# Hybrid decoder trunk on one core: expert rows added to the output in DRAM by accumulating scatters, and a third probability buffer in attention

## The chip, the core and the metric

The kernel runs on one core of a Trainium2 chip. The core has a matrix engine (PE, TensorE), a vector engine (DVE), an activation engine (ACT), GpSimd (POOL), a queue engine for transfers (SP) and 16 DMA engines. The metric is the device time of one execution in microseconds; less is better. POOL's indirect DMAs take one index per partition and move one row of DRAM for each.

## The reference

Two layers over 1024 tokens of width 1024, float32. Cut to what matters:

```python
for l in range(DEPTH):                                   # DEPTH = 2
    z = rms_norm(x, norm1_gain[l]) @ w_in[l]             # q | k | v | u, 512 columns each
    q, k = per-head RMSNorm, partial rotary              # 8 heads of 64
    att = dilated_attention(q, k, v)                     # causal, a count mask, softmax
    pool = pool_mixer(u, w_pool[l], pool_scale[l])
    x = x + concat(att, pool) @ w_out[l]
    h = rms_norm(x, norm2_gain[l])
    x = x + hier_moe(h, ...)     # each token goes to 2 of 16 SwiGLU experts (256 wide), with weights
```

## The kernel before

Tokens lie in T = 8 tiles of 128 (`x_res`, called `xr` in the code). One program runs over both layers in a hardware loop. Each engine has its own instruction stream, in order, written out by hand; semaphores tie them. Stages of a layer:

- **Input projection.** PE turns normalised x and multiplies with `w_in`, first q and v for the 8 tiles, then k and u. ACT squares a tile (`square_x`), DVE makes the factor and scales (`norm_x`), PE transposes (`xt`), DVE applies the gain and splits it into a high and a low part (`gain1`). A projection of a tile and half is 24 matmuls (L1321). For the second layer the first of this is done inside the last stage of the layer before.
- **Attention.** 8 heads x 8 row tiles = 64 steps m. PE `scores(m)` (L1381, L1383), DVE `mask(m)` (L1025: adds the mask, finds the row maximum, writes buffer `pr[m % 2]`), ACT `exp(m)` (L730, in place), PE `probs_t(m)` transposes (L1301), ACT and DVE copy the turned blocks from PSUM (L748, L1035), PE `probs_v(m)` multiplies with 128 columns of v, those of two heads (L1407), DVE `over_sum(m)` divides the 64 columns of its head (L1041, L1044). `mask(m)` waits until `probs_t(m - 2)` is done. At steps 3 and 11 of every 16, DVE splits q and k of the next head (`q_and_k_low`, L1000, L1003); ACT writes the high part of k twice (L673, L677).
- **Output projection**, residual into `xr`; ACT writes the normalised rows to `token_rows` in DRAM. Then the **router**, whose sorting is done by DVE and by small float16 matmuls (L1504).
- **Experts.** Tokens are sorted by expert into blocks of 128 rows. There is room for BLOCKS = 31; the first layer uses 22, the second 23, a number known at run time (`used`), and the engines branch past the rest one by one. For block t POOL gathers rows (L579), PE transposes, multiplies with gate and up (L1527) and down (L1540). ACT and DVE copy y to SBUF, and ACT writes it to `y_table` in DRAM (L816). POOL also gathers for the unused blocks.
- **Combination.** After the last block POOL gathers two rows of `y_table` per token (L595, 16 gathers per layer) and DVE adds them into `xr` with the token's weights (L1267, L1269). In layer 2 POOL then writes `xr` to the output (L601).

The instructions at the end of a layer's expert stage are these:

```python
for t in range(T):
    if t >= GATHS:
        pool.wait_ge(x_ready, upto(l + 1, T, t - GATHS + 1))
        pool.sem_inc(s_passed, 1)
    for k in range(2):
        pool.indirect_dma_start(
            out=gath[t % GATHS][:, k, :], out_offset=None,
            in_=y_table, in_offset=bass.IndirectOffsetOnAxis(ap=pos_i[:, k, t:t + 1], axis=0),
        ).then_inc(s_gath[t % GATHS], 16)
```

## Time and profile before

| | |
|---|---|
| median of 3 runs | 1771.88 us (1771.16 to 1774.53) |
| the profiled execution: its own time, its span | 1771.18 us, 1769.1 us |
| PE busy | 1488.7 us, 84% |
| DVE busy | 829.6 us, 47% |
| ACT busy | 470.7 us, 27% |
| POOL busy | 273.9 us, 15% |
| moved by DMA | 228.42 MB, mean 129 GB/s |
| mean granted TensorE clock | 0.932 of full |

The span runs from the first to the last instruction. The shares are means over stages with different limits. Input projection, output projection and expert blocks keep PE near full; the attention leaves some of its time, and two stretches without much PE work stand at the end of each layer's expert stage.

### The profile page before, as it was taken

How to read it: one execution, taken by the hardware profiler on the slowest of the kernel's cores; microseconds unless marked ns; L12 is line 12 of the kernel's file. 1: busy time of each engine (PE TensorE's matmuls, PEld its weight loads, DVE VectorE, ACT ScalarE, POOL GpSimd, SP SyncE). 2: the span in 40 equal slices, each digit the busy share in tenths (PEclk: the TensorE clock that was granted, in tenths of full speed). 3: DMA queues.
4: the chain of work that ended last, by engine and by line, in shares of the span. 5: the costliest groups of instructions: out<-in, count | busy, mean ns of one | idle time of the engine just before them, and what ended most of it. 6: DMA issues, size and time to landing. Idle time of an engine off the chain costs nothing.

```text
span 1769.1 us, 23000 instructions
## 1 busy us (share of the span) xinstructions
PE 1488.7 (84%) x6931; PEld 1068.9 (60%) x6932; DVE 829.6 (47%) x2097; ACT 470.7 (27%) x904; POOL 273.9 (15%) x259
## 2 busy tenths in 40 slices
PE   2999987998992999998269999789999659999960
PEld 2887867886882444444158787678778524444430
DVE  3778667664436112221377866766634441222114
ACT  3222155763111011111212313566512101111100
POOL 1200049002001001110310000940200020111114
PEclk8999989999995999999579999899999869999985
DMA  8410020000057588942740002000001935888637
GB/s 304 154 43 1 0 96 1 1 1 1 36 179 260 173 297 290 367 155 83 246 166 0 1 0 81 16 1 1 1 13 48 329 99 196 293 294 297 226 128 288
DMA packets 118497, 228.42 MB, mean 129 GB/s; under 512 B 6184, under 2 KB 72816, under 8 KB 118416
## 3 DMA queue, kind: packets, MB, share of 16 engines
q1 hardware_dynamic: 90352, 129.55, 21.5%
q0 software_dynamic: 18128, 65.71, 10.4%
q10 hardware_dynamic: 9936, 32.14, 4.5%
q8 instruction: 44, 0.72, 0.2%
q14 instruction: 37, 0.30, 0.1%
HBM read 183.33 MB, written 44.04 MB: 129 GB/s over the span
## 4 chain that ended last, share of the span: by engine, by line
PE 71%; DVE 11%; issue 8%; DMA 4%; ACT 4%; ACTq 0%; POOL 0%; DVEq 0%; PEld 0%; POOLq 0%; SPq 0%; PEldq 0%
PE ps L1527 18%; PE ps L1321 17%; PE ps L1301 9%; PE ps L1454 9%; PE ps L1540 8%; PE ps L1407 4%; PE ps L1468 2%; DMA arena<-token_rows,next_tok 1%; DMA big<-y_table,pos_i 1%; DVE arena L1025 1%; DVE w_in_lo L920 1%; ACT arena L730 1%; ACT arena L748 1%; DVE arena L1122 1%; PE ps L1381 1%
## 5 line engine op out<-in xcount | busy, mean ns | idle before, releaser
L1301 PE MATMUL ps<-cst,arena 128*128 128x128 f32 x1682 | 244.5, 282 | 128.5 <-DVE arena L891 59.8
L1527 PE MATMUL ps<-big,arena 128*128 x720 | 326.3, 607 | 11.0 <-issue 10.5
L1301 PEld LDWEIGHTS ps<-cst,arena 128*128 128x128 f32 x1682 | 201.3, 145 | 206.8 <-DVE arena L891 61.9
L881 DVE TENSOR_TENSOR arena<-ps,par 128x512 f32<-128x512 f32 x126 | 81.2, 686 | 365.5 <-PE ps L1301 365.3
L1527 PEld LDWEIGHTS ps<-big,arena 128*128 128x128 f32 x720 | 135.9, 194 | 172.5 <-issue 172.5
L1321 PE MATMUL ps<-w_in_hi,hT_hi 128*128 128x512 f32 x512 | 207.1, 404 | 12.3 <-DVE w_in_lo L920 8.6
L1321 PE MATMUL ps<-w_in_hi,hT_lo 128*128 128x512 f32 x512 | 203.0, 396 | 0.0
L1321 PE MATMUL ps<-w_in_lo,hT_hi 128*128 128x512 f32 x512 | 202.9, 396 | 0.0
L1540 PE MATMUL ps<-big,arena 128*128 x360 | 165.3, 603 | 7.0 <-issue 7.0
L1407 PE MATMUL ps<-big,arena 128*128 128x128 f32 x1152 | 150.6, 276 | 0.0
L1407 PEld LDWEIGHTS ps<-big,arena 128*128 128x128 f32 x1152 | 140.0, 193 | 1.3
L578 POOL COPY next_tok<-row_tok 128x1 int32 (+1 forms) x62 | 14.8, 238 | 781.0 <-PE ps L1301 452.2
L730 ACT ACTIVATE arena<-arena,st 128x128 f32<-128x128 f32 (+7 forms) x128 | 99.1, 774 | 82.1 <-DVE st L1025 81.2
L1321 PEld LDWEIGHTS ps<-w_in_hi,hT_hi 128*128 128x128 f32 x512 | 98.8, 193 | 34.8 <-DVE w_in_lo L920 10.4
L1025 DVE CUSTOM_DVE_ANT_0 arena<-ps,cst 128x128 f32<-128x128 f32 (+7 forms) x128 | 96.5, 754 | 44.7 <-PE ps L1301 40.7
L1321 PEld LDWEIGHTS ps<-w_in_hi,hT_lo 128*128 128x128 f32 x512 | 98.2, 192 | 21.4
L1540 PEld LDWEIGHTS ps<-big,arena 128*128 128x128 f32 x360 | 66.1, 194 | 73.9 <-issue 73.9
L1321 PEld LDWEIGHTS ps<-w_in_lo,hT_hi 128*128 128x128 f32 x512 | 98.6, 193 | 19.6
L1454 PE MATMUL ps<-w_o_hi,cat_hi 128*128 128x512 f32 x256 | 102.9, 402 | 7.4 <-DVE cat_lo L1087 7.4
L1454 PE MATMUL ps<-w_o_hi,cat_lo 128*128 128x512 f32 x256 | 100.3, 392 | 0.0
L1454 PE MATMUL ps<-w_o_lo,cat_hi 128*128 128x512 f32 x256 | 100.2, 391 | 0.0
L1381 PE MATMUL ps<-k_high,q_parts 128*128 128x512 f32 (+1 forms) x192 | 82.0, 427 | 12.0 <-DVE k_low L1003 11.8
(159 smaller groups left out, 1749.5 us busy)
## 6 DMA issues: line engine op xcount, KB each, us to landing
big<-in_w_gate SPq DMA_DIRECT2D x32, 1024.0 KB, 8.8
big<-in_w_up SPq DMA_DIRECT2D x32, 1024.0 KB, 11.3
big<-in_w_down SPq DMA_DIRECT2D x32, 1024.0 KB, 13.5
y_table<-arena ACTq DMA_DIRECT2D x45, 512.0 KB, 6.8
big<-in_w_in SPq DMA_DIRECT2D x18, 1024.0 KB, 10.4
big<-in_w_out SPq DMA_DIRECT2D x4, 2048.0 KB, 10.1
token_rows<-arena ACTq DMA_DIRECT2D x16, 512.0 KB, 2.8
y_table<-x_res POOLq DMA_DIRECT2D x15, 512.0 KB, 9.5
```

Of the source, the lines that this page charges most:

```text
L730: sc.activation(pr[b][:, 0:nk], pr[b][:, 0:nk], ACT.Exp, scale=-1.0, bias=st[:, 64 + m % 16:65 + m % 16], accum_out=st[:, 80 + m % 16:81 + ...
L748: sc.activation(prT[b][:, 0:nb, :], ps[:, 4, 0:nb * P] .rearrange("p (a c) -> p a c", c=P), ACT.Copy).then_inc(pt0_ev, 1)
L881: ins = ve.tensor_tensor(out=dst[:, 4 * h:4 * h + 4, :], in0=ps[:, banks + h, :].rearrange("p (a c) -> p a c", c=P), in1=spread(gain[:, 4 ...
L1025: ve.tensor_tensor_reduce(out=pr[b][:, 0:nk], in0=ps[:, 2 * b:2 * b + 2, :].rearrange("p a c -> p (a c)")[:, 0:nk], in1=cst[:, C_MASK + SE ...
L1301: ins = te.transpose(ps[:, bank + i // 4, (i % 4) * P:(i % 4 + 1) * P], src, ident)
L1321: ins = te.matmul(ps[:, 2 + 2 * par_ + i, :], a[par_][:, k, :], b[:, k, :], start=k == 0 and n == 0, stop=k == K - 1 and n == 2)
L1381: te.matmul(ps[:, 2 * b + c // 512, 0:w], q_parts[a][:, i * P:(i + 1) * P], k_high[a][:, c:c + w], start=True, stop=False)
L1407: ins = te.matmul(ps[:, 6 + b, 0:P], prT[b][:, j, :], v[:, j, p * P:(p + 1) * P], start=j == 0, stop=j == i)
L1454: ins = te.matmul(ps[:, 2 * par_ + h, :], a[par_][:, k, :], b[:, k, :], start=k == 0 and n == 0, stop=k == K - 1 and n == 2)
L1468: ins = te.matmul(ps[:, 6 + par_, 0:P], h2T[par_][:, k, :], wr_all[:, ds(l * (K * NR) + k * NR, P)], start=k == 0, stop=k == K - 1)
L1527: ins = te.matmul(ps[:, 2, :], xgT[:, k, :], big[:, ds(at + k * 2 * FE, 2 * FE)], start=k == 0, stop=k == K - 1)
L1540: ins = te.matmul(ps[:, 4 + h, :], aT[:, k, :], big[:, ds(at + (E_GU + k * D + 512 * h), 512)], start=k == 0, stop=k == 1)
```

## The change

Four things change together.

1. `y_table` and the combination go. While the output projection runs, ACT also writes each tile of x to the output in DRAM. For each block j POOL issues `add_rows(j)`: an indirect DMA that adds the 128 rows of y to the rows of their tokens in the output (rows without a token go to spare rows behind it). It stands 5 blocks after the gather in POOL's order, for all 31 blocks. Since a token has two experts, `y_whole` lets the add of a used block start only after the one before it has landed. The weights go into the experts: DVE cuts the weights into three parts of 11 bits, 16 float16 matmuls of 96 columns sort them by row, and `act` is multiplied by them.
2. The gathered rows `xg` and `y` now lie in tiles 2 to 7 of `xr`. For layer 2 SP loads tiles 0 and 1 of x from the output after the add of the last block with tokens has landed (`x_whole`), and tiles 2 to 7 after all 31 adds.
3. Attention has three `pr` buffers, so that `mask(m)` waits for `probs_t(m - 3)`. `probs_v` multiplies with the 64 columns of its own head, and the 8 tiles of a head lie in one PSUM bank; `over_sum` runs once per head, on 512 columns.
4. The second copy of k's high part moves from ACT to DVE. `in_low(l + 1, 0)` moves behind the first `rows_evac`.

```diff
-GATHS = 4
+AHEAD = 5
+OUT_ROWS = SEQ + ROWS
-        att = A[:, 2048:3072].rearrange("p (t c) -> p t c", c=P)
+        att = kT_r.rearrange("p (a t c) -> p a t c", a=PAIRS, c=P)
-        pr = ring(5120, SEQ)
+        pr = ring(5120, SEQ) + [A[:, 2048:3072]]
-        xg = ring(0, D, RING)
+        xg = [xr[:, 2 + i, :] for i in range(RING)]
-        y = ring(4864, D, RING)
+        y = [xr[:, 2 + RING + i, :] for i in range(RING)]
...
+                with sp.If(l > 0):
+                    sp.wait_ge(x_whole, upto(l, 1, 0))
+                    sp.sem_inc(s_passed, 1)
+                    for t in range(2):
+                        sp.dma_start(xr[:, t, :], out[t * P:(t + 1) * P, :]).then_inc(s_again[t], 16)
+                    for t in range(2):
+                        sp.wait_ge(s_again[t], l * 16)
+                        sp.sem_inc(x_ready, 1)
...
+                    sp.wait_ge(s_add, upto_added(l, 0))
+                    sp.sem_inc(s_passed, 1)
+                    for t in range(2, T):
+                        sp.dma_start(xr[:, t, :], out[t * P:(t + 1) * P, :]).then_inc(s_again[t], 16)
...
-                    ch.link(nc.gpsimd.tensor_copy(next_tok[:, slot:slot + 1], row_tok[:, ds(j, 1)]))
                     pool.indirect_dma_start(
                         out=xg[slot], out_offset=None, in_=token_rows,
-                        in_offset=bass.IndirectOffsetOnAxis(ap=next_tok[:, slot:slot + 1], axis=0)).then_inc(s_xg[slot], 16)
+                        in_offset=bass.IndirectOffsetOnAxis(ap=row_tok[:, j:j + 1], axis=0)).then_inc(s_xg[slot], 16)
+                def add_rows(j):
+
+                    pool.wait_ge(y_whole, upto(l, BLOCKS, j + 1))
+                    pool.sem_inc(s_passed, 1)
+                    pool.indirect_dma_start(
+                        out=out, out_offset=bass.IndirectOffsetOnAxis(ap=row_dst[:, j:j + 1], axis=0),
+                        in_=y[j % RING], in_offset=None, compute_op=ALU.add).then_inc(s_add, 16)
...
+                for j in range(BLOCKS):
+                    load_rows(j, j % RING, j // RING)
+                    if j >= AHEAD:
+                        add_rows(j - AHEAD)
+                for j in range(BLOCKS - AHEAD, BLOCKS):
+                    add_rows(j)
+            pool.wait_ge(s_add, upto_added(DEPTH, 0))
...
+                    a_.dma_start(out[ds(t * P, P), :], xr[:, t, :]).then_inc(s_base, 16)
...
                     a_.wait_ge(y1_ready, upto(l, BLOCKS, t + 1))
-                    a_.dma_start(y_table[ds(t * P, P), :], y[slot]).then_inc(s_y[slot], 16)
+                    if not first(t):
+                        a_.wait_ge(s_add, upto_added(l, t))
+                    a_.sem_inc(y_whole, 1)
...
                         moe_down(t, slot, m)
+                        a_.wait_ge(s_add, upto_added(l, t + 1))
+                        a_.sem_inc(x_whole, 1)
                     with a_.Else():
                         a_.sem_inc(y1_ready, 1)
-                        a_.sem_inc(s_y[slot], 16)
+                        a_.sem_inc(y_whole, 1)
...
-                                     in1=k_high[a][own, :].bitcast(f32), op=ALU.subtract).then_inc(staged, 1)
+                                     in1=k_high[a][own, :].bitcast(f32), op=ALU.subtract)
+                    ve.tensor_copy(k_high[a][other, :], kT[own, p, :]).then_inc(staged, 1)
...
-                    if m >= 2:
-                        j = m - 2
+                    if m >= 3:
+                        j = m - 3
...
+                    ve.tensor_tensor(out=att[:, p, :, HD * a:HD * (a + 1)],
+                                     in0=ps[:, 6 + a, :].rearrange("p (t c) -> p t c", c=HD),
+                                     in1=spread(r, HD), op=ALU.mult).then_inc(o_ev, 1)
...
-                        ins = te.matmul(ps[:, 6 + b, 0:P], prT[b][:, j, :], v[:, j, p * P:(p + 1) * P],
-                                        start=j == 0, stop=j == i)
+                        ins = te.matmul(ps[:, 6 + hd % 2, i * HD:(i + 1) * HD], prT[b][:, j, :],
+                                        v[:, j, hd * HD:(hd + 1) * HD], start=j == 0, stop=j == i)
```

Engine POOL, end of a layer's expert stage, before: the last gather of an unused block, then the gathers of the combination.

```order
L574 REGISTER_ALU
L575 ISA
L578 COPY next_tok<-row_tok 128x1
L579 DMA arena<-token_rows,next_tok 128x1024
L588 ISA x2
L595 DMA big<-y_table,pos_i 128x1024 x8
L592 ISA
L595 DMA big<-y_table,pos_i 128x1024 x2
```

The same place of the change; L607 is the gather, L615 the accumulating scatter (its index buffer is in the arena), L613 a wait for `y_whole`.

```order
L603 REGISTER_ALU
L607 DMA x_res<-token_rows,row_tok 128x1024
L615 DMA out_x<-x_res,arena 4992x1024
L603 REGISTER_ALU
L604 REGISTER_ALU
L607 DMA x_res<-token_rows,row_tok 128x1024
L615 DMA out_x<-x_res,arena 4992x1024 x3
L613 REGISTER_ALU
L615 DMA out_x<-x_res,arena 4992x1024
```

The copy of the index and the 16 gathers of `y_table` are gone, and every gather but the first five has a scatter behind it.

Engine DVE, attention, from the mask of a row tile of 256 columns to that of 512 columns, before: each step has a reciprocal and a product of 64 columns.

```order
L1025 ISA arena,st<-ps,cst 128x256
L1025 ISA st 128x1
L1041 RECIPROCAL st<-st 128x1
L1044 TENSOR_SCALAR arena<-ps,st 128x64
L1023 REGISTER_ALU
L1025 ISA arena,st<-ps,cst 128x384
L1025 ISA st 128x1
L1041 RECIPROCAL st<-st 128x1
L1044 TENSOR_SCALAR arena<-ps,st 128x64
```

The same stretch of the change, up to the division of the head before.

```order
L1044 ISA arena,st<-ps,cst 128x256
L1044 ISA st 128x1
L1042 REGISTER_ALU
L1044 ISA arena,st<-ps,cst 128x384
L1044 ISA st 128x1
L1042 REGISTER_ALU
L1044 ISA arena,st<-ps,cst 128x512
L1044 ISA st 128x1
L1061 RECIPROCAL st<-st 128x8
L1063 TENSOR_TENSOR big<-ps,st 128x8x64
```

Sixteen small instructions of a head have become two.

Engine PE, attention, the products with v between two scores, before and then in the change: only the shape of the moving operand differs, from 128 to 64 columns.

```order
L1301 MATMUL ps<-cst,arena 128x128 x4
L1395 REGISTER_ALU
L1301 MATMUL ps<-cst,arena 128x128 x4
L1407 MATMUL ps<-big,arena 128x128 x7
L1377 REGISTER_ALU
```

```order
L1332 MATMUL ps<-cst,arena 128x128 x4
L1426 REGISTER_ALU
L1332 MATMUL ps<-cst,arena 128x128 x4
L1438 MATMUL ps<-big,arena 128x64 x7
L1408 REGISTER_ALU
```

The number of matmuls and their place among the others stay.

## Rows read from the trace of the kernel before

**Rows 1.** Busy time by stretch: length; PE, PEld, DVE, ACT, POOL; clock; DMA.

```profile
238.00:408.00 170.00, 144.07 (x1066) 129.44 (x1065) 113.42 (x306) 112.07 (x227) 67.37 (x31) 0.97 0.05 20
571.50:830.20 258.70, 254.24 (x740) 122.48 (x740) 49.49 (x87) 28.45 (x64) 25.16 (x44) 0.99 0.66 234
830.20:916.50 86.30, 32.31 (x109) 23.79 (x110) 41.80 (x78) 15.63 (x24) 21.05 (x26) 0.67 0.55 193
1706.00:1769.10 63.10, 5.12 (x8) 2.03 (x8) 21.45 (x18) 1.24 (x3) 24.56 (x32) 0.58 0.68 251
```

**Rows 2.** Chain that ended last, by time, between the layers: start, length, what.

```profile
842.08 9.87 DMA arena<-token_rows,next_tok
...
855.30 8.20 DMA big<-y_table,pos_i
...
916.45 12.75 PE ps L1321 x48
```

**Rows 3.** Timeline between the layers: start, length, engine, line, operation.

```profile
839.38 0.60 ACT L813 ACTIVATE arena<-ps 128x512 f32<-128x512 f32 x1 [7.55 <-PE ps L1540]
...
840.65 0.96 POOL L579 DMA_INDIRECT arena<-token_rows,next_tok  x1 [0.50 <-POOL next_tok L578]
...
847.03 1.28 ACT L852 ACT_TABLE_LOAD   x1 [7.04 <-DVEq L1248]
...
866.17 1.06 ACT L625 ACTIVATE arena<-x_res 128x1024 f32<-128x1024 f32 x1 [17.64 <-DVE x_res L1269]
...
875.33 0.79 PE L1321 MATMUL ps<-w_in_hi,hT_hi 128*128 128x512 f32 x1 [3.67 <-DVE hT_lo L909]
```

**Rows 4.** The chain in layer 1, from the second half of tile 0 on.

```profile
43.19 12.49 PE ps L1321 x48
57.00 10.91 PE ps L1321 x48
```

**Rows 5.** Timeline of the end of layer 2.

```profile
1716.03 0.96 POOL L579 DMA_INDIRECT arena<-token_rows,next_tok  x1 [0.50 <-POOL next_tok L578]
```

**Rows 6.** Stretches near the end, columns as in rows 1.

```profile
1732.00:1740.00 8.00, 0.00 (x0) 0.00 (x0) 7.11 (x6) 0.00 (x0) 4.58 (x5) 0.50 1.01 397
...
1757.00:1761.00 4.00, 0.00 (x0) 0.00 (x0) 0.00 (x0) 0.00 (x0) 0.00 (x0) 0.50 0.60 247
```

**Rows 7.** DMA issues of the page: count, KB each, median us to landing.

```profile
y_table<-arena ACTq DMA_DIRECT2D x45, 512.0 KB, 6.8
...
x_res<-in_x SPq DMA_DIRECT2D x1, 512.0 KB, 3.3
arena<-token_rows,next_tok POOLq DMA_INDIRECT x62, 5.9
```

**Rows 8.** Groups of the attention of layer 1 (240 to 408 us): busy, mean ns.

```profile
L1407 PE MATMUL ps<-big,arena 128*128 128x128 f32 x546 | 71.5, 276 | 0.0
L1407 PEld LDWEIGHTS ps<-big,arena 128*128 128x128 f32 x546 | 66.3, 193 | 0.6
...
L1044 DVE TENSOR_SCALAR arena<-ps,st 128x64 f32<-128x64 f32 x62 | 17.6, 284 | 18.8 <-DVE st L1041 14.8 <-PE ps L1407 2.5
...
L1003 DVE TENSOR_TENSOR k_low<-big,k_high 64x1024 fp32r<-64x1024 f32 x8 | 12.1, 1513 | 0.1
...
L1041 DVE RECIPROCAL st<-st 128x1 f32<-128x1 f32 x62 | 9.8, 158 | 0.0
```

**Rows 9.** What PE waited for there: total us, times, longest.

```profile
PE ps L1301 <- ACT arena L748: 11.2, 21, 1.1
PE ps L1381 <- DVE k_low L1003: 5.9, 1, 5.9
PE ps L1301 <- DVE arena L1035: 5.9, 2, 3.1
```

**Rows 10.** Timeline: products with v, and weight loads of the float16 matmuls.

```profile
315.33 1.95 PE L1407 MATMUL ps<-big,arena 128*128 128x128 f32 x16
...
559.53 0.29 PEld L1504 LDWEIGHTS ps<-arena 128*128 128x128 f16 x8 [11.05 <-DVE arena L1200]
```

More of the change, by code:

```diff
@@ L98, in shape_constants @@
     c[:, C_JJ:C_JJ + P] = np.arange(P)
-    c[:, C_TOK:C_TOK + 2 * T] = np.tile(P * np.arange(T), 2)[None, :] + row
+    c[:, C_TOK:C_TOK + 2 * T] = np.tile(P * np.arange(T), 2)[None, :] + row + 1
     c[:, C_DESC:C_DESC + 4] = 4 - np.arange(4)
@@ L104, in shape_constants @@
     c[:, C_INV:C_INV + 16] = 1.0 / (1.0 + np.arange(16))
+    c[:, C_SPARE:C_SPARE + 32] = SEQ + 1 + P * np.minimum(np.arange(32), BLOCKS - 1)[None, :] + row
     return c
@@ L189, in trunk @@
                 for i in range(SLOTS)]
-        gath = [big[:, AT_K + 2 * D * i:AT_K + 2 * D * (i + 1)].rearrange("p (k n) -> p k n", k=2) for i in range(GATHS)]
         def ring(at, size, n=2, inner=None):
@@ L291, in trunk @@
         routed = sem("routed")
+        gate_parts = sem("gate_parts")
+        gates_listed = sem("gates_listed")
+        y_whole = sem("y_whole")
+        x_whole = sem("x_whole")
         w_loaded = sem("w_loaded")
@@ L320, in trunk @@
         s_xg = [sem(f"s_xg{i}") for i in range(RING)]
-        s_y = [sem(f"s_y{i}") for i in range(RING)]
-        s_gath = [sem(f"s_gath{i}") for i in range(GATHS)]
-        s_out = sem("s_out")
+        s_base, s_add = sem("s_base"), sem("s_add")
+        s_again = [sem(f"s_again{t}") for t in range(T)]
         s_ms = sem("s_ms")
@@ L509, in _ @@
                         .then_inc(s_wr, 16)
-            for j in range(2 * SEQ // P, BLOCKS):
-                pool.dma_start(y_table[j * P:(j + 1) * P, :], xr[:, 0, :]).then_inc(s_fill, 16)
             with pool.Fori(0, DEPTH) as l:
@@ L608, in _ @@
             for s in (params, q_high_in, k_high_in, win_top, gain_in, sd1, sqz_done, sdz, cat_top, v_copied, u_copied, t_evac, p_ready, pt0_ev, at_ev, sd2,
-                      ge_exp, dm_exp, silu_done, aT_ready, y1_ready):
+                      ge_exp, dm_exp, silu_done, aT_ready, y1_ready, y_whole, x_whole):
                 a_.sem_inc(s, BIAS)
-            for s in s_y + s_tok:
+            for s in s_tok:
                 a_.sem_inc(s, 1)
@@ L672, in k_top @@
                     own, other = heads(a)
-                    sc.activation(k_high[a][own, c], kT[own, p, c], ACT.Copy)
-                def k_top_again(p, a, c=slice(0, SEQ)):
-                    own, other = heads(a)
-                    sc.activation(k_high[a][other, c], kT[own, p, c], ACT.Copy).then_inc(k_high_in, 1)
+                    sc.activation(k_high[a][own, c], kT[own, p, c], ACT.Copy).then_inc(k_high_in, 1)
                 def in_act(t, par_, h):
@@ L749, in _ @@
                                   .rearrange("p (a c) -> p a c", c=P), ACT.Copy).then_inc(pt0_ev, 1)
-                    if p and n == 1:
+                    if p and n == 3:
                         att_evac(p - 1)
@@ L1055, in _ @@
                         mask(m + 2)
-                    if m >= 1:
-                        over_sum(m - 1)
+                    if m >= T and m % T == 1:
+                        over_sum(m // T - 1)
                     if n == 3:
@@ L1215, in _ @@
                 dve.sem_inc(s_passed, 1)
+                dve.wait_ge(s_base, (l + 1) * (16 * T))
+                dve.sem_inc(s_passed, 1)
+                bits = gate_w[:, :, :].rearrange("p k t -> p (k t)").bitcast(i32)
+                ve.tensor_scalar(gate_bits[:, 0, :], bits, 0x7FF, None, ALU.bitwise_and)
+                ve.tensor_scalar(gate_bits[:, 1, :], bits, 11, 0x7FF, ALU.logical_shift_right, ALU.bitwise_and)
+                ch.link(ve.tensor_scalar(gate_bits[:, 2, :], bits, 22, None, ALU.logical_shift_right))
+                ch.link(ve.tensor_copy(R("parts"), gate_bits[:, :, :].rearrange("p k c -> p (k c)")))
+                parts = R("parts").rearrange("p (k c) -> p k c", k=3)
+                tt(R("tmp3", 32), spread(R("blk"), 32), count, ALU.is_equal)
+                for k in range(3):
+                    ins = ve.tensor_tensor(out=in_gate[:, :, k, :], in0=R("tmp3", 32), in1=spread(parts[:, k, :], 32),
+                                           op=ALU.mult)
+                ins.then_inc(gate_parts, 1)
+                ch.link(ve.tensor_scalar(R("spare"), ps[:, 2, 0:32], 0.0, None, ALU.is_equal))
+                tt(R("spare"), R("spare"), cst[:, C_SPARE:C_SPARE + 32], ALU.mult)
+                ch.link(ve.scalar_tensor_tensor(out=row_dst[:, :], in0=ps[:, 2, 0:32], scalar=-1.0, in1=R("spare"),
+                                                op0=ALU.add, op1=ALU.add))
                 used = dve.value_load(start_i[0:1, NE:NE + 1], min_val=2 * SEQ // P, max_val=BLOCKS)
@@ L1544, in _ @@
                 xtm(0, 0, 0)
+                pe.wait_ge(gate_parts, upto(l, 1, 1))
+                for c in range(2 * T):
+                    ins = te.matmul(ps[:, 7, 0:96], in_row[:, c, :], in_gate[:, c, :, :].rearrange("p k b -> p (k b)"),
+                                    start=c == 0, stop=c == 2 * T - 1)
+                ins.then_inc(gates_listed, 1)
                 used = pe.value_load(start_i[0:1, NE:NE + 1], min_val=2 * SEQ // P, max_val=BLOCKS)
```

149 lines of the change are left out of this document (64 added, 85 removed).

## The prediction, made before the change ran

> **What bounds the kernel now.** I read the stretches first. In the expert blocks PE is busy 254 of 259 us [rows 1], so nothing that other engines save there counts; 22 blocks in 258.7 us are 11.8 us a block, and layer 2 has 23. In the attention PE is busy 144 of 170 us, at a clock of 0.97. Two stretches hold hardly any PE work: 830 to 916 us, between the layers, with 32 of 86 us, and 1706 us to the end, with 5 of 63. Together they last 149 us, and the change works there. Next the chain of waits and the timeline say what these stretches wait for. After the last copy of y (839.4 us) come gathers for unused blocks (842.1 us, 9.9 us to land), a gather of y (855.3 us, 8.2 us), and x is complete when ACT squares it at 866.2 us; the first projection of layer 2 starts at 875.3 us, and the run of 48 matmuls that begins with the second half of tile 1 only at 916.5 us [rows 2, 3]. In layer 1 the run before it starts at 43.2 and this one at 57.0 us, 13.8 us apart [rows 4].
>
> **The gap between the layers.** The last y is copied at 840.0 us. POOL issues the pending gather, now without the copy of its index (840.0 to 841.2; an issue is 0.96 us plus about 0.3 between two), then the scatter of block 21. The trace has no accumulating transfer. Its landing I bound from the write of y (6.8 us) and the gather that took 9.9 us at this very place beside a weight load [rows 2, 7]; I take 8.8, so 850 us. Then ACT sets `x_whole`. SP's loads of tiles 0 and 1 need 3.3 us and a little [rows 7], about 855. But ACT now waits for the scatter before it branches past the unused blocks. That took the 7.0 us between its copy of y and the table load, less about 0.5 to issue the write of y, so 6.5, and lay under the gathers [rows 3]; now it is in the open: 856.5, table load 1.3 and a first operation 0.2, square at 858.0 instead of 866.2. The first projection follows 9.2 us later as before, at 867.2. It takes 7.2 us at the low clock, the transposes 2.0, so the second half of tile 0 starts at 876.4. DVE no longer has 16 additions of 1.28 us between its steps, so I put the spacing of layer 1, 13.8 us, behind it: 890.2 instead of 916.5, a gain of 26 us.
>
> **Tiles 2 to 7 wait for all 31 scatters.** Tile 2 is wanted at about 883, 7 us before that. Nine scatters of unused blocks and three gathers are left at 850. POOL needs 12 x 1.24 = 15 us to issue them. What a scatter occupies of the DMA engines, E, decides more. The engines moved 397 GB/s when full [rows 6]: 512 KB are 1.3 us for a plain copy, the lower end. An add has to read the old row too: twice, 2.6 us. The upper end is the 6.8 us in which a write of y lands [rows 7], as if they went one by one. I take 2.6, nearest to the rows with full engines, since the nine need not wait for each other. Then 851 + 9 x 2.6 + 3 x 1.3 = 878.3, tile 2 at 881.6: just in time, 0 us. At E = 1.3 nothing changes; at 6.8 the last lands at 916, and tile 2 at 919 puts the run at 926, 10 us worse than before.
>
> The Trainium skill (Collectives: The Full Stack, The bandwidth ceiling) says that an add in a DMA engine is slower than a copy not by the addition but by its two source reads, and puts the ratio at two. By it E is 2.6; no row here shows an add, so the sum stands on the bounds above.
>
> **The end.** The last block's scatter is issued behind one gather, at 1716.7 us (the gather stands at 1716.0 now and loses its copy) [rows 5], and lands at about 1723. Eight scatters of unused blocks at 2.6 follow: 1744. Before, data stopped at 1757 + 0.6 x 4 = 1759.4 and the span at 1769.1, 9.7 us later [rows 1, 6]; the same behind 1744 gives 1754, a gain of 15. At E = 1.3 the issues bound it (10 x 1.24, plus 3 to land): 1748, a gain of 21. At 6.8: 1723 + 54 + 10 = 1787, a loss of 18.
>
> **Attention, DVE and ACT.** Gone are 64 reciprocals of 158 ns and 64 products of 284 ns with 18.8 us of idle before them [rows 8], 47 us of DVE's stream per layer; eight divisions of 512 columns (about 0.9 us each with the reciprocal) and eight copies of 64 x 1024 (at most 1.5, as L1003) come back, 19 us. DVE is not the bound, so this counts only where PE waits: 23 us per layer [rows 9]. The 5.9 us before the first score stay and grow by the copy, up to 1.5 us, which ACT had made earlier. The 5.9 us for the copy L1035 come from DVE standing in `q_and_k_low`; the third buffer does not help there. The 11.2 us in 21 waits for ACT's copy do: that copy stands behind `exp(m + 1)`, which waited for a mask that waited for `probs_t(m - 1)`. I take 9.5 of them. Net 8 us per layer, 16 in all; bounds 0 and 23 per layer. The output of attention moves off the arena, which costs nothing.
>
> **Attention, PE.** The product with v streams 64 columns instead of 128. Now 16 of its instructions take 1.95 us, (1.95 - 0.276)/15 = 112 ns apart [rows 8, 10], and 576 per layer are 64 us. If the moving operand sets this, it may halve, 53 ns each, 31 us per layer. If the weight load does, nothing is won. A float32 load lasts 193 ns, and eight float16 loads together 290 ns at the lower clock [rows 8, 10]: a load has a short fixed part, so most of 193 ns is loading, and it fills the 112. I take 0; bounds 0 and 61 us in all.
>
> The Trainium skill (TensorE: Matmul & The Clock Gate, LDWEIGHTS (loading the stationary operand)) gives columns / 1.2 ns, 107 ns for 128 columns whatever the matmul's width. [...]
>
> **The start of the experts.** 16 matmuls of 96 columns come between the first transposes and the first gate matmul: at 1.2 GHz 80 ns each, 1.3 us, plus a wait for DVE's parts, less the index copy that the first gather loses: +1 us per layer, 2 in all. DVE's cutting of the weights (about 4 us) lies under the first gather. The write of x by ACT lies under the output projection. In the blocks the add of one block must land before the next starts: issue and landing of 5.9 to 9.9 [rows 2, 7] fit in 11.8, so 0. POOL's wait for `y_whole` holds up a gather that is wanted three blocks later. If the cover is gone, each us over 11.8 costs 45.
>
> **Sum.** -26 - 15 - 16 + 2 = -55 us against the profiled execution's own 1771.2 (its median of runs is 0.7 higher): **1716 us**.
>
> **Rivals.**
> - *The moving operand sets the pace in attention.* For: the stream is continuous and both explanations give 112 ns. Against: the 193 ns load. Then up to 61 us more: 1655 to 1680. Chance 0.12.
> - *Scatters occupy the engines longer, E = 3.5 to 5.8.* For: the nearest landings are 6 to 7 us. Nine and eight of them stand in the open, so each us of E costs 17: 1731 to 1770. Chance 0.16.
> - *Slower than before.* The same mechanism from E = 5.9 on, where 17 x (E - 2.6) exceeds 55; at 6.8 it gives 1787, and from a landing above 11.8 us the blocks themselves stretch by 45 us per us. Against: full engines moved 397 GB/s. Chance 0.08.
> - *The clock falls in attention*, since half the columns pass; 0.97 now [rows 1]. It was granted 0.5 in stretches without PE work [rows 6]. If a tenth of the 2 x 144 us of PE work ran at 1.2 GHz instead of 2.4, it would cost 29 us: 1745. Chance 0.05.
> - *The tail is not shortened*, because 31 scatters are issued whatever is used: that is the E = 4.5 case, counted above.
> - Forecast, E below 3.5 and no gain on PE: 1698 to 1735. Chance 0.59.
>
> The range reaches from the first rival's middle to the slow scatters' upper part: 1670 to 1758. About 0.2% (3.5 us) is what a measurement can tell from no change. Faster 0.90, within it 0.02, slower 0.08.
>
> **What would show it.** Right: no PE work between about 840 and 867, the square of layer 2 near 858 behind ACT's branches, the run of 48 matmuls near 890; scatters at the end spaced under 3 us and a last stretch of about 48 us; products with v still 112 ns apart; the mask's waits shorter. Wrong: tile 2 of x arriving after 883, ACT waiting for an add inside the blocks, or products with v closer than 100 ns.

## The result, and the profile after

The changed kernel takes 1753.75 us, the median of five executions (1741.32 to 1757.35), against 1771.88: a ratio of 0.9885, 95% interval 0.9867 to 0.9903. So it is faster, by 18 us where 55 were forecast. The profiled execution is the fastest of the five, 1741.3 us (span 1739.4); the working below is held against this one, 29.7 us less span than before. Seven more executions of the same kernel follow in the experiments. All twelve fall into two groups, 1734.6 to 1742.1 (5) and 1750.8 to 1757.4 (7), where all executions of the kernel before (1766.2 to 1774.8) lie within 9 us. That needs a cause of its own.

Busy time by stretch of the kernel after, the same stretches and columns as [rows 1]: attention of layer 1, its expert blocks, the gap, the end.

```profile
238.00:408.00 170.00, 149.15 (x1054) 137.52 (x1052) 102.24 (x199) 103.37 (x217) 63.91 (x31) 0.90 0.05 18
575.00:830.00 255.00, 249.25 (x732) 120.48 (x733) 54.25 (x87) 28.49 (x63) 52.01 (x41) 0.99 0.78 235
830.00:897.90 67.90, 31.95 (x118) 22.50 (x117) 23.01 (x64) 15.66 (x24) 27.82 (x17) 0.72 0.85 225
1676.00:1739.40 63.40, 16.48 (x47) 7.38 (x45) 3.75 (x6) 2.94 (x6) 22.24 (x16) 0.69 0.67 141
```

The gap has shrunk from 86 us to 68. In the attention DVE is relieved (102 us for 113), but PE is busy for 149 us instead of 144, and its mean clock is 0.90 instead of 0.97: PE was made slower, not shorter of work.

I cut both spans at the same events, read from the timelines (start of the first window sum behind the attention, of the last down projection of each layer, of the run of 48 matmuls in [rows 2], end of the last matmul of the projection of layer 2):

| event | before | after | shift |
|---|---|---|---|
| end of layer 1's input projection | 239.9 | 238.9 | -1.0 |
| first window sum, layer 1 | 413.0 | 414.7 | +1.7 |
| last down projection, layer 1 | 826.5 | 829.4 | +2.9 |
| run of 48, layer 2 | 916.5 | 897.9 | -18.6 |
| end of layer 2's input projection | 1101.2 | 1080.8 | -20.4 |
| first window sum, layer 2 | 1275.0 | 1260.4 | -14.6 |
| last down projection, layer 2 | 1702.0 | 1685.8 | -16.2 |
| end | 1769.1 | 1739.4 | -29.7 |

The gap gave 21.5 us (forecast 26), the end 13.5 (15). The two attentions, 173.1 and 173.8 us before, took 175.9 and 179.6: 8.6 us more where 16 less were forecast. That is the miss of this execution.

The chain of the kernel after between the layers (answers to [rows 2]), by start and length:

```profile
829.42 3.45 PE ps L1571 x8
843.87 11.32 DMA out_x<-x_res,arena
...
872.58 8.19 PE ps L1352 x24
...
889.63 4.30 issue
897.88 10.92 PE ps L1352 x48
```

Its timeline there ([rows 3]); the last row is an issue of an add that took 5.88 us:

```profile
856.93 1.58 POOL L615 DMA_INDIRECT out_x<-x_res,arena  x1 [10.20 <-ACTq L851]
...
862.02 1.28 ACT L870 ACT_TABLE_LOAD   x1 [20.02 <-ACTq L850]
...
863.43 1.04 ACT L650 ACTIVATE arena<-x_res 128x1024 f32<-128x1024 f32 x1
...
872.37 5.88 POOL L615 DMA_INDIRECT out_x<-x_res,arena  x1 [0.31 <-issue]
```

The mechanism is the forecast's, a few us late at each step: the last real add lands at 855.2 instead of 850, ACT's square stands at 863.4 instead of 858.0, the first projection at 872.6 instead of 867.2. Tiles 2 to 7 of x come only at some 889, because POOL's first add of an unused block (856.9) waits for ACT's branch, and that for the landing. The sum let these adds start at 850, before ACT had branched.

The end, two rows of POOL's timeline and one of the stretches ([rows 5, 6]):

```profile
1707.94 1.59 POOL L615 DMA_INDIRECT out_x<-x_res,arena  x1 [6.40 <-ACTq L851]
...
1723.66 1.56 POOL L615 DMA_INDIRECT out_x<-x_res,arena  x1 [0.30 <-issue]
...
1730.00:1735.00 5.00, 0.00 (x0) 0.00 (x0) 0.00 (x0) 0.00 (x0) 0.00 (x0) 0.50 1.01 201
```

The engines are full with adds until 1735, 10 us behind the last issue, and move 201 GB/s of payload (182 to 234 in the four stretches of 5 us before), where full engines moved 397 in [rows 6]. By this estimate a 512 KB add occupies all engines for 512 KB / 201 GB/s = 2.6 us: the value taken for E. POOL issues one every 1.87 us, so the engines, not POOL, set the end. The Trainium skill (Collectives: The Full Stack, The bandwidth ceiling) has an add at half a copy's rate; this trace agrees in the main, 201 against 397 GB/s.

In the attention of layer 1 (238 to 408 us), the groups that answer to [rows 8], and the product of 16 of [rows 10]:

```profile
L1438 PE MATMUL ps<-big,arena 128*128 128x64 f32 x546 | 73.6, 284 | 0.0
L1438 PEld LDWEIGHTS ps<-big,arena 128*128 128x128 f32 x546 | 72.1, 207 | 0.7 <-issue 0.2
...
L1023 DVE CAST k_high<-big 64x1024 fp32r<-64x1024 f32 x8 | 11.6, 1453 | 0.1
L1063 DVE TENSOR_TENSOR big<-ps,st 128x512 f32<-128x512 f32 x7 | 4.8, 691 | 0.2
...
338.91 1.90 PE L1438 MATMUL ps<-big,arena 128*128 128x64 f32 x16
```

With half the columns a product still follows the last one after (1.90 - 0.284)/15 = 108 ns (112 before): the weight load sets the pace, so the edit gives PE nothing. What PE waited for (238 to 412 us; answers to [rows 9]):

```profile
PE ps L1332 <- DVE arena L1054: 7.0, 2, 5.3
PE ps L1412 <- DVE k_high L1023: 6.9, 1, 6.9
PE ps L1332 <- ACT arena L765: 4.7, 10, 1.1
```

The waits for ACT's copy fell from 11.2 to 4.7 us. All three together fell from 23.0 to 18.6, and still the attention got 2.8 us longer, so some 7 us went into PE's own work. Stretches of 20 us of the kernel after, two of layer 1 and one of layer 2, show where:

```profile
255.00:275.00 20.00, 17.17 (x98) 16.01 (x96) 10.92 (x18) 7.64 (x18) 18.99 (x11) 0.71 0.00 1
275.00:295.00 20.00, 14.71 (x83) 13.50 (x83) 15.02 (x19) 8.65 (x18) 19.06 (x8) 0.76 0.00 1
...
1155.00:1175.00 20.00, 20.00 (x99) 18.79 (x98) 6.95 (x15) 8.92 (x20) 0.00 (x0) 0.59 0.00 1
```

The next to last column is the DMA share; the one before it the clock. The kernel before had 1.00 and 1.00 in the first two (with 140 and 122 matmuls instead of 98 and 83) and 0.91 at its lowest in layer 2. In the last, PE never stood still and was granted 0.59 of full speed, mostly the lower of its two levels (1.2 instead of 2.4 GHz).

### The profile page after: what moved, and what is told of

It reads as the page before. It is cut to its first block, busy times and chain, and to the rows that moved or that the text cites. A ratio compares the mean times of both kernels' runs of the same rounds, so it can differ in the third digit from the quotient of the medians.

```text
span 1739.4 us, 22561 instructions
## 1 busy us (share of the span) xinstructions
PE 1495.3 (86%) x6963; PEld 1085.7 (62%) x6964; DVE 781.9 (45%) x1883; ACT 454.6 (26%) x886; POOL 314.4 (18%) x204
## 4 chain that ended last, share of the span: by engine, by line
PE 77%; DVE 9%; issue 6%; DMA 3%; ACT 2%; ACTq 1%; POOL 1%; DVEq 0%; SPq 0%; PEld 0%; PEldq 0%; POOLq 0%
PE ps L1558 18%; PE ps L1352 18%; PE ps L1332 10%; PE ps L1485 10%; PE ps L1571 9%; PE ps L1438 6%; PE ps L1412 2%; PE ps L1499 2%; PE ps L1414 2%; DMA out_x<-x_res,arena 1%; DVE k_high L1023 1%; DVE arena L1141 1%; DMA big<-in_w_in 1%; PE ps L1472 1%; DVE w_in_lo L938 1%
## 5 line engine op out<-in xcount | busy, mean ns | idle before, releaser
L1558 PE MATMUL ps<-big,arena 128*128 x720 | 320.5, 598 | 9.8 <-issue 8.4
L1332 PE MATMUL ps<-cst,arena 128*128 128x128 f32 x1242 | 186.6, 285 | 87.3 <-DVE arena L909 46.0
L1558 PEld LDWEIGHTS ps<-big,arena 128*128 128x128 f32 x720 | 133.8, 191 | 167.3 <-issue 167.3
L1332 PEld LDWEIGHTS ps<-cst,arena 128*128 128x128 f32 x1242 | 152.8, 147 | 134.3 <-DVE arena L909 47.6
L607 POOL DMA_INDIRECT x_res<-token_rows,row_tok x62 | 61.0, 984 | 599.2 <-issue 307.7
L1571 PE MATMUL ps<-big,arena 128*128 x360 | 163.8, 598 | 5.4 <-issue 5.4
L1438 PE MATMUL ps<-big,arena 128*128 128x64 f32 x1152 | 154.9, 284 | 0.0
L1438 PEld LDWEIGHTS ps<-big,arena 128*128 128x128 f32 x1152 | 151.9, 207 | 1.5 <-issue 0.4
L615 POOL DMA_INDIRECT out_x<-x_res,arena x62 | 102.7, 1656 | 170.4 <-ACTq L832 140.3
L1571 PEld LDWEIGHTS ps<-big,arena 128*128 128x128 f32 x360 | 65.5, 192 | 71.5 <-issue 71.5
```

The costliest lines, as they stand in the source:

```text
L607: pool.indirect_dma_start(out=xg[slot], out_offset=None, in_=token_rows, in_offset=bass.IndirectOffsetOnAxis(ap=row_tok[:, j:j + 1], axis= ...
L615: pool.indirect_dma_start(out=out, out_offset=bass.IndirectOffsetOnAxis(ap=row_dst[:, j:j + 1], axis=0), in_=y[j % RING], in_offset=None, ...
L1332: ins = te.transpose(ps[:, bank + i // 4, (i % 4) * P:(i % 4 + 1) * P], src, ident)
L1438: ins = te.matmul(ps[:, 6 + hd % 2, i * HD:(i + 1) * HD], prT[b][:, j, :], v[:, j, hd * HD:(hd + 1) * HD], start=j == 0, stop=j == i)
L1558: ins = te.matmul(ps[:, 2, :], xgT[:, k, :], big[:, ds(at + k * 2 * FE, 2 * FE)], start=k == 0, stop=k == K - 1)
L1571: ins = te.matmul(ps[:, 4 + h, :], aT[:, k, :], big[:, ds(at + (E_GU + k * D + 512 * h), 512)], start=k == 0, stop=k == 1)
```

## The experiments

Two theories. **A, the clock:** the products with v stream half the columns, the granted clock falls in the first heads, and this eats the gain. **B, DVE held up beside POOL:** while POOL sums windows and cuts the output weights in the first heads, DVE's pieces of q and k take longer; the change gave DVE one more such piece per head (the copy of k's high part), and PE waits. A third reading, that the scatters or the new end cost the time, is a rival to both. Medians are of five to eight executions unless said; ratios are against the kernel before, run beside them on the same chip (medians 1770.2 to 1772.2).

**1. The changed kernel again** (no edit).

> The changed kernel once more, unedited, for a second profile and the spread of its times. Theory A (the clock falls in attention, because the products with v stream half the columns and PE pauses more): median 1747 to 1755 us, the executions 10 us or more apart, and in the new profile again stretches of the attention at a granted clock under 0.9, not necessarily the same ones. Theory B (fixed stalls in attention, from the second copy of k's high part on DVE): the attention lasts 182 and 186 us again, with the same waits at the same heads, whatever the clock. If the spread comes from the end or the gap instead, the attention is alike in both profiles and the last stretch differs by 10 us.

Median 1739.6 us (1734.6 to 1753.7), ratio 0.9839 (0.9802 to 0.9875). The median lies under A's 1747 to 1755, the executions are 19 us apart as A had it, and B's 182 and 186 us are missed. Clock 0.82, 0.86 and 0.97 from 255 to 315 us, 0.75 in one stretch of layer 2. The attentions took 171.2 and 173.7 us, together 2.0 us less than before, and yet this execution lasted as long as the profiled one above: from the first window sum to the last down projection it took 6.9 us more in the two layers, all of it before the first down projections, where the clock in layer 2 was 0.87 instead of 0.89. The low clock comes again and its depth varies. It lies in the heads beside POOL's work or just behind it: in layer 2 POOL has stopped at 1149.7 us, and the stretch from 1155 to 1175 us has 0.88.

**2. k's second copy back on ACT.** The changed kernel, with

```
-                    ve.tensor_copy(k_high[a][other, :], kT[own, p, :]).then_inc(staged, 1)
...
+                    if n == 10:
+                        k_top_again(p + 1, 0)
```

> The changed kernel with the second copy of k's high part back on ACT. Theory A (clock, from the 64-column products): the waits for that copy go (about 3 to 5 us per layer), the clock still falls somewhere in the attention, the time stays at 1743 to 1755 with the same spread. Theory B (the copy on DVE, stretched from 0.7 to 4 us beside POOL's conversions, stalls PE and the pause then lowers the clock): the attention comes down to about 172 us per layer, the forecast's 8 us of gain, total about 1725 to 1735, spread under 4 us.

1745.5 us (1740.5 to 1760.9), ratio 0.9863: within A's 1743 to 1755, B's 1725 to 1735 missed, the spread stayed. The attentions took 176.5 and 176.1 us, where B had 172. Its timeline in layer 2 shows why the copy is not all of it, DVE and POOL side by side:

```profile
1142.54 9.82 DVE L1031 TENSOR_TENSOR k_low<-big,k_high 64x1024 fp32r<-64x1024 f32 x1
...
1141.53 9.75 POOL L583 TENSOR_TENSOR w_o_lo<-big,w_o_hi 128x4096 fp32r<-128x4096 f32 x1
```

A subtraction of 1.22 us (its length elsewhere) that starts 1 us behind POOL's subtraction of 4096 columns ends 1.1 us after it. The subtraction can be caught as the copy can.

**3. Only the 64 columns, in the kernel before.**

```
-    te.matmul(ps[:, 6 + b, 0:P], prT[b][:, j, :], v[:, j, p * P:(p + 1) * P], ...)
+    te.matmul(ps[:, 6 + b, HD * a:HD * (a + 1)], prT[b][:, j, :],
+              v[:, j, p * P + HD * a:p * P + HD * (a + 1)], ...)
```

> The kernel before with one edit: the products with v write 64 columns instead of 128. Theory A (half the columns let the clock fall): slower than before, 1776 to 1790, with stretches of the attention under 0.9 of the clock that were at 1.00. Theory B: the clock stays as it was; 2 x 576 products are 4 ns closer (108 instead of 112), at most 4.6 us less: 1767 to 1772.

1781.7 us (1779.7 to 1787.7), ratio 1.006 (1.0047 to 1.0074): 9.5 us **slower** than before. Its profiled execution is 14.2 us over that of before, and its attentions (177.6 and 183.6 us) account for 14.3 of it. PE's waits did not grow (2.7 us for DVE's copy in layer 1, 5.9 before). Two of its stretches of 20 us:

```profile
275.00:295.00 20.00, 16.03 (x87) 14.64 (x85) 12.44 (x26) 7.46 (x17) 18.99 (x9) 0.71 0.00 1
...
1175.00:1195.00 20.00, 19.73 (x86) 18.65 (x86) 7.13 (x25) 9.54 (x21) 0.00 (x0) 0.50 0.01 2
```

This shows A by itself, and the time is in A's 1776 to 1790: no scatter, no third buffer, no copy on DVE, and the clock falls.

**4. Only the scatters.** The changed kernel with the whole attention as before (two buffers, 128 columns, division by row, k's copy on ACT).

> The changed kernel with the whole attention as it was before (two probability buffers, 128-column products, division by row, k's copy on ACT): only the scatters and the early load of x remain. Both theories: the gap between the layers keeps its 21 us and the end its 13, the attention is 180 us per layer at a clock of 1.00 again: 1733 to 1738, spread under 4 us. If the scatters' DMA traffic or the new expert blocks cost something that I have missed, or if the spread comes from them, it is 1741 or more, or the executions are 10 us apart.

1738.4 us (1737.5 to 1741.9), ratio 0.9812 (0.9799 to 0.9825). The scatters give 34 us in all executions alike (forecast 39 for these parts), and the spread is 4.4 us. So the scatters cause neither the loss nor the two groups, and the change of the attention is worth nothing in the lower group and costs 15 us in the upper.

**5 and 6. 128 columns again, with two and with three buffers.** The changed kernel; the surplus 64 columns are overwritten by the next row's product:

```
-    te.matmul(ps[:, 6 + hd % 2, i * HD:(i + 1) * HD], prT[b][:, j, :], v[:, j, hd * HD:(hd + 1) * HD], ...)
+    n = HD if i == T - 1 or hd == HEADS - 1 else 2 * HD
+    te.matmul(ps[:, 6 + hd % 2, i * HD:i * HD + n], prT[b][:, j, :], v[:, j, hd * HD:hd * HD + n], ...)
```

> The changed kernel with products with v that stream 128 columns again (the 64 too many are overwritten by the next row's product; in row 7 and head 7 it stays 64), and with two probability buffers instead of three. Against the run of the 128 columns with three buffers it prices the third buffer alone: by the forecast's reading (9.5 us per layer of waits for ACT's copy) it is 15 to 19 us slower than that run, about 1735 to 1740; if the division by head was what mattered, the two are within 4 us.

> The changed kernel, three probability buffers, division by head, k's copy on DVE, and only the products with v streaming 128 columns again (row 7 and head 7 stay at 64). Theory A (the clock fell for the halved columns): the granted clock is 0.95 or more in every stretch of 20 us behind the first one of the attention, both attentions last 172 to 177 us, total 1718 to 1724, spread under 6 us: faster than either kernel. Rival (fixed stalls from DVE's copies beside POOL, or the new order of rows): the clock stays low between 255 and 295 us and the time is 1735 to 1745.

Two buffers: 1738.0 us (1735.1 to 1740.4). Three: 1734.7 (1726.4 to 1739.5), ratio 0.9801 (0.9781 to 0.9822), attentions of 170.9 us each, clock 0.91 or more behind 255 us. A's direction held, its size did not: 1718 to 1724 was expected. The third buffer is worth 3 us per layer by the two profiles (attentions of 173.7 and 174.1 without it) and 3.3 us in both layers together by the medians, not 9.5 per layer. And PE's wait for ACT's copy is 5.3 us with two buffers and 5.2 with three, from 11.2: the division by head removed that wait, not the buffer (the copy on DVE alone left 9.4 of it in experiment 16).

**7. POOL's work of the attention held back until row 32 of 64**, in the changed kernel:

```
+                pool.wait_ge(s_done, upto(l, 16 * PAIRS, 32))
                 for g in range(NG):
                     pool_group(g)
```

> The changed kernel, 64 columns, with POOL's work of the attention (sums over windows, cutting of the output weights, some 62 us) held back until row 32 of 64. If PE pauses because DVE is slowed beside POOL, the first heads get a clock of 1.00 and a copy of k in 0.7 us, and the slowed copies and the clock under 0.9 move to the stretch from 315 to 375 us. If the low clock of the first heads comes from the way the attention starts (behind a stretch at low clock), it stays at 255 to 295 us and the later stretch stays at 1.00. Total 1735 to 1755 either way; slower if POOL's work then ends behind the attention.

1731.3 us (1729.1 to 1733.0), ratio 0.9771, 4 us under the expected range. The low clock moved with POOL's work: 1.00 in the first heads, where k's copies now take 0.69 us, and then (315 to 335, 355 to 375 us)

```profile
315.00:335.00 20.00, 17.12 (x133) 15.50 (x131) 13.59 (x23) 12.64 (x28) 18.98 (x11) 1.00 0.00 1
...
355.00:375.00 20.00, 19.32 (x89) 18.26 (x90) 6.47 (x18) 9.02 (x18) 19.30 (x6) 0.53 0.01 1
```

In this run the clock fell where both came together: the narrow products, and the pauses that PE makes where POOL is at work. In the other stretches behind the first the narrow products kept 0.95 or more. That is not a rule for all runs: in experiment 2 the clock was 0.91 and 0.83 in two stretches (335 to 355, 375 to 395 us) in which POOL did nothing. Over all profiles the columns divide more clearly. Wherever the products had 64 columns, some stretch of 20 us behind the first 20 us of an attention was granted 0.50 to 0.75; with 128 columns none was granted less than 0.83.

**8. Unused blocks move 16 rows**, in the kernel of experiment 4:

```
+                    with pool.If(used > j):
+                        body(j, P)
+                    with pool.Else():
+                        body(j, 16)
```

> The kernel with the scatters alone (attention as before), in which a gather and a scatter of an unused block move 16 rows instead of 128, by a branch on POOL. If POOL's issues (1.87 us apart at the end) grow with the rows, the end gets about 10 to 12 us shorter and the loads of tiles 2 to 7 of x come 7 us or more earlier, of which up to 7 count: 1719 to 1728 against 1738. If an issue costs the same whatever its rows, and POOL has branches besides: 1736 to 1745.

1728.1 us (1725.0 to 1733.3), ratio 0.9765 (0.9747 to 0.9783): 10.3 us less than in 4. The issues came only from 1.87 to 1.6 us apart; what went is the transfer behind them. At the end DMA is now slack:

```profile
1710.00:1715.00 5.00, 0.00 (x0) 0.00 (x0) 0.00 (x0) 0.00 (x0) 3.67 (x3) 0.50 0.44 48
```

**9, 10 and 11. Combinations.** 9 is 6 and 7 together, 10 is the one edit of 7 in the kernel before, 11 is 9 with the edit of 8.

> The changed kernel with both remedies: products with v on 128 columns and POOL's work of the attention held back until row 32. With 64 columns and POOL late the clock was 1.00 until POOL began and 0.53 for one stretch of 20 us behind it, in both layers. If half the columns and POOL's pauses are both needed for a fall, the clock is now 0.95 or more in all stretches, each attention lasts 163 to 168 us (170.8 with the fall), total 1718 to 1723, spread under 6 us. If the fall comes from POOL's pauses alone, it stays at 350 to 400 us and the time is 1728 to 1733.

> The kernel before, only POOL's work of the attention held back until row 32. If the place of POOL's work matters by itself (DVE's first pieces of k and q, 2.8 us instead of 1.2 beside POOL, stand in the open at the start), this gains 2 to 4 us per layer: 1764 to 1768. If it is the new order of rows or the smaller number of DVE's operations that brings the gain seen with POOL late, this is 1769 to 1774.

> The changed kernel with three edits: 128 columns, POOL late, and 16 rows instead of 128 for the gathers and scatters of unused blocks (which took 10.3 us off the kernel with the scatters alone). If these add up: 1708 to 1714. If the shorter end and the earlier loads of x were worth less behind the changed attention: 1714 to 1722.

9: 1728.5 us (1724.7 to 1730.5), ratio 0.9765 (0.9744 to 0.9785); attentions of 167.4 and 167.8 us as expected, the total 5 us over. With 128 columns the fall is gone in the stretch that had 0.53 in experiment 7:

```profile
355.00:375.00 20.00, 17.27 (x135) 15.96 (x136) 13.59 (x25) 13.61 (x28) 19.39 (x5) 1.00 0.00 1
```

10: 1763.2 us (1760.1 to 1764.6), ratio 0.9954 (0.9939 to 0.9969): moving POOL's work helps the kernel before by 7 us too, 1 us more than its 1764 to 1768 allowed. 11: 1719.8 us (1718.7 to 1724.4), ratio 0.9719, above its 1708 to 1714. Against the profile of 9 the path from the last down projection of layer 1 to the end of the next input projection is 6.6 us shorter and the end 8.5 us, but from the first window sum to the first down projection it takes 8.9 us more in the two layers, in layer 2 at a clock of 0.87 instead of 0.89. Why the clock is lower there no run takes apart.

**12. The changed kernel once more**, for a profile of the upper group.

> The changed kernel once more, unedited, for one more profile. Its eleven times so far lie in two groups, 1734.6 to 1742.1 (5) and 1750.8 to 1757.4 (6), with both profiles in the lower one. If this falls in the upper group, the theory of the clock expects one more stretch of 20 us or so at a clock near 0.5 in one of the attentions and nothing else changed; if the two groups come from the scatters, the end or the gap is 10 us longer.

1752.65 us. The first attention took 186.1 us (171.2 in experiment 1), the second 173.7 in both: more than the 10.6 us between the two executions. DVE, POOL and PE of this run:

```profile
293.50 9.20 DVE L1023 CAST k_high<-big 64x1024 fp32r<-64x1024 f32 x1
...
292.49 9.66 POOL L583 TENSOR_TENSOR w_o_lo<-big,w_o_hi 128x4096 fp32r<-128x4096 f32 x1
...
303.07 0.69 PE L1332 MATMUL ps<-cst,arena 128*128 128x128 f32 x2 [13.23 <-DVE arena L1054]
```

The copy needs 0.69 us alone. Here it starts 1 us behind POOL's longest operation, ends 0.6 us behind it, and PE stands for 13.2 us; the subtraction just before it had taken 4.52 us instead of 1.22. This is what theory B describes. But the low clock that I had expected is there as well:

```profile
275.00:295.00 20.00, 14.84 (x75) 13.22 (x74) 12.65 (x13) 7.37 (x15) 18.99 (x9) 0.76 0.00 0
295.00:315.00 20.00, 11.93 (x80) 11.66 (x81) 12.83 (x15) 7.08 (x15) 10.95 (x3) 0.67 0.00 1
```

The same stretches had 0.86 and 0.97 in experiment 1. PE's waits for DVE's copy L1054 grew from 3.8 to 15.0 us there, 11.2 of the 14.9 us by which this attention is longer. The rest goes with the lower clock, part of which came before the standstill.

**13 to 16. The two causes apart.** 13: the changed kernel with 128 columns and k's copy on ACT. 14: the changed kernel, POOL's cutting in pieces,

```
-                split_out(0, 0, K * 512).then_inc(wo_split, 1)
+                for c in range(0, K * 512, 512):
+                    ins = split_out(0, c, c + 512)
+                ins.then_inc(wo_split, 1)
```

and the second half alike.

15: experiment 11 with these pieces. 16: the kernel before with k's second copy on DVE, behind `k_low`, instead of on ACT.

> The changed kernel with 128 columns and with k's second copy on ACT. Theory A (the fallen clock is the main loss): as the run with 128 columns alone, 1730 to 1736. Theory B (a piece of DVE's that starts beside a long operation of POOL's ends only with it, 9.2 us instead of 0.7 in the profile with the longer attention): one piece less per head can be caught, so about 2 to 4 us less, but two of three pieces are still there and the spread stays at 8 us or more.

> The changed kernel, 64 columns, k's copy on DVE, and POOL cuts the output weights in pieces of 512 columns instead of one of 4096 (subtraction about 1.2 us instead of 9.7). Theory B (the upper group of the times, 1751 to 1757, is DVE's copy caught behind POOL's long subtraction): no piece of DVE's is held longer than some 3 us there, the upper group is gone, all executions within 8 us at 1732 to 1742. Theory A alone (the clock's fall makes the two groups): both groups stay, 14 us apart.

> The changed kernel with 128 columns, POOL late, 16 rows for unused blocks, and POOL's cutting in pieces of 512 columns. Without the pieces the median was 1719.8 and each attention 167.3 to 167.9 us. If the pieces free DVE in the two heads beside POOL's cutting: 1714 to 1719, attention 165 to 167. If POOL's more and shorter operations cost as much in links between them: 1718 to 1722.

> The kernel before, 128 columns, two buffers, with k's second copy on DVE behind the two subtractions instead of on ACT. Theory B: slower than before in some or all executions, 1774 to 1786 with a spread of 8 us or more, and a copy of 3 us or more beside POOL. If the copy costs its 0.7 us each only: 1771 to 1774, the spread of before.

13: 1738.4 us (1732.1 to 1740.3), no better than 6 and above both expectations; in this attention, divided by head, the copy is as well on DVE. Its profiled execution took 1737.0 us although DVE's subtraction was caught in both layers, for 9.83 and 9.84 us. In layer 1:

```profile
296.60 9.83 DVE L1031 TENSOR_TENSOR k_low<-big,k_high 64x1024 fp32r<-64x1024 f32 x1
...
306.81 0.69 PE L1341 MATMUL ps<-cst,arena 128*128 128x128 f32 x2 [5.33 <-DVE arena L1063]
```

So PE waits 5.3 us for the one caught piece, and that doesn't by itself make an execution of the upper group; in experiment 12 two pieces in a row were held up, and the products were narrow.

14: 1740.1 us (1733.3 to 1746.7), ratio 0.9822 (0.9799 to 0.9845). No copy lasted over 2.8 us and none of the six executions lies above 1746.7, so the upper group is gone as far as six can tell; but the executions are 13 us apart instead of 8, and the profiled one has

```profile
295.00:315.00 20.00, 19.27 (x93) 18.13 (x93) 6.90 (x18) 8.87 (x20) 12.46 (x14) 0.58 0.01 1
```

and a first attention of 179.9 us with only 4.1 us of waits for DVE's copy L1057 (the second took 168.3 us). Cause A is left; that it makes the whole of the remaining spread is not shown. 15: **1709.1 us** (1707.5 to 1714.0), ratio 0.9654 (0.9636 to 0.9672), the fastest of all and 5 us under what was expected, attentions of 163.4 and 163.1 us. 16: 1782.7 us (1779.5 to 1784.3), ratio 1.0065 (1.0051 to 1.008), with these waits of PE in the attention of layer 1:

```profile
PE ps L1292 <- DVE arena L1026: 12.7, 7, 4.4
PE ps L1292 <- ACT arena L742: 9.4, 14, 1.1
PE ps L1372 <- DVE k_high L995: 6.9, 1, 6.9
```

Before it was 5.9, 11.2 and 5.9 [rows 9], together 6.0 us less. The copy alone costs 11.8 us in two layers, as theory B had it, but not by being caught: no copy lasted over 2.3 us, and the executions are 5 us apart.

## Why the prediction was wrong, step by step

- **What fails is the step "Attention, PE", with "Attention, DVE and ACT".** The first put the 64 columns at 0 with bounds "0 and 61 us in all", all of it gain. That the load sets the pace was right (108 ns apart). But the bound on the other side was missing: with the same number of loads and half the columns the clock falls, +9.5 us in the kernel before (experiment 3). It stood among the rivals with a chance of 0.05 and was then left out of the sum. The measured time lies in the stated 1670 to 1758 only by luck: the upper part of that range was there for slow scatters, which did not come.
- **The 8 us per layer.** The copy on DVE was priced at up to 1.5 us once, at the first score; experiment 16 measured 5.9 us per layer. The wait before the first score grew by 1.0 us, and PE's waits for `half_evac`, queued behind `q_and_k_low`, grew by 6.8 us in layer 1, 3.8 of them in the heads beside POOL (up to 315 us) and 3.0 behind, where there had been none; the waits for ACT's copy fell by 1.8. That 5.9 us of wait "from DVE standing in `q_and_k_low`" was in the sum as unchanged, though the edit makes that very stay longer by a third piece. The 9.5 us of waits for ACT's copy went by 6.5, through the division by head; the third buffer gives at most 3 us per layer more (experiments 5 and 6), and in layer 1 the waits for DVE's copy fell with it from 10.3 to 8.7 us.
- **What each has cost in the profiled execution:** the attentions' +8.6 instead of -16 are 24.6 us, nearly the whole of the 25.3 us between -55 and -29.7 (the gap's 4.5 and the end's 1.5 are made up elsewhere). In experiment 1, as fast, the attentions are 14 us off the forecast and the rest of the miss lies outside them. The median is further off by 12 us, because seven of twelve executions fall in the upper group. The one profile of that group shows DVE's pieces held up behind POOL and a low clock together (12), and without the long operations of POOL the group did not come (14).
- **The gap**, -26: -21.5. Right mechanism. The add took 11.3 us to land instead of 8.8, the adds of unused blocks began behind ACT's branches, and POOL needed 1.58 us to issue one where the sum had 0.96. Experiment 8 shows what they cost: with an eighth of the rows in their gathers and adds, 10.3 us less at the gap and the end together.
- **The end**, -15: -13.5, right, with E = 2.6 as taken: the engines set it, so that POOL's longer issues did not count. All rivals that rested on a larger E (0.24 together) fell with it; so did the one that the moving operand sets the pace (0.12), by the 108 ns.
- **The start of the experts**, +2: the first gate matmuls came 4.1 us later in layer 1 at 575.7, but at a warmer clock (7.1 us for the first run instead of 9.05), and the last down projection only 2.9 us later. About 0. The output projection, which the sum did not name, started at a low clock and cost 2.5 us in layer 1 (13.67 us for its first 48 matmuls, 11.20 before). Inside the blocks of layer 1 ACT waited for an add once, for 0.4 us.

Open stays how much of the clock's fall comes from the columns and how much from PE's pauses. A fall under 0.83 behind the first 20 us of an attention was seen with narrow products alone, so they are needed for it in these runs; what else must come to it, and how deep it then goes, no run takes apart. Also open is why the copy on ACT does not help the changed kernel (2 and 13) though on DVE it costs the kernel before so much (16); DVE's stream is shorter once the division goes by head, but no run took that apart.

## What to carry to other kernels

Where the weight load sets the pace of matmuls, narrowing the moving operand gained nothing here and let the clock fall: look at the granted clock in the stretches that already pause, and price that side too. Before giving DVE a piece of work, look for long POOL operations beside it: a short DVE operation that starts behind one may end only behind it (9.2 us for 0.69), so cut POOL's work in pieces or put it where DVE has least to do. When the execution times of one kernel fall in two groups, profile until there is one of each: here that showed how far a collision can hold PE up (13.2 us).

## What the runs showed of the hardware

- A DVE operation beside a POOL tensor_tensor of two float32 inputs can take as long as the rest of POOL's: 9.20 us for a copy of 0.69 (experiment 12), 9.82 for a subtraction of 1.22 (experiment 2). They end 0.6 and 1.1 us behind POOL's end, nearly their whole own length, so DVE got hardly anything done beside it. The Trainium skill (SBUF — State Buffer, Who interferes with whom) has DVE and GpSimd share a pair of ports under an exclusive lock, held for a whole instruction; the traces agree in these cases.
- I had not expected a granted clock of 0.59 in a stretch where PE was busy all 20 us (kernel after, layer 2), beside 1.00 in one where it was busy for 17.1 (experiment 7). Once fallen, the clock stayed low through most of a stretch in which PE no longer paused.
- An accumulating scatter of 512 KB in DRAM occupied the 16 engines for an estimated 2.6 us, by 201 GB/s where copies had 397; on the chain it landed 6.1 to 11.3 us after its issue. POOL needs 1.58 us to issue one of 128 rows, 1.30 for one of 16.
